# Retrieval spread over eight tiles a head instead of nine, with ScalarE's share written as a loop

## The reference

```
q = (ht @ w_q).reshape(T, 8, 2, 128)                  # 8 heads
s1, s2 = q[:, :, 0] . k1, q[:, :, 1] . k2              # 128 scores each
v1, i1 = top_k(s1, 16); v2, i2 = top_k(s2, 16)
cand = v1[..., :, None] + v2[..., None, :]             # 256 candidates
sc, flat = top_k(cand, 16)
idx = i1[flat // 16] * 128 + i2[flat % 16]
gate = softmax(sc)
act = gelu(x . u_tab[idx]); out = (gate * act) . v_tab[idx]
```

## Time and profile before

| what | value |
|---|---|
| median of three runs | 1848.8 us (1847.82 to 1850.55) |
| the profiled execution, its own time | 1851.15 us |
| its span | 1849.5 us |
| PE busy | 1812.2 us, 98% |
| DVE busy | 1423.3 us, 77% |
| ACT busy | 895.1 us, 48% |
| POOL busy | 513.9 us, 28% |

### The profile page before, as it was taken

The page is one execution under the profiler, slowest core; times in us unless marked ns, Lnnn a source line. Parts: engine busy times, 40 slices in busy tenths (PEclk is TensorE's granted clock), DMA queues, the critical chain, the costliest instruction groups (busy, mean ns, idle before and its releaser), DMA issues.

```text
span 1849.5 us, 37505 instructions
## 1 busy us (share of the span) xinstructions
PE 1812.2 (98%) x13425; PEld 1680.1 (91%) x13425; DVE 1423.3 (77%) x2638; ACT 895.1 (48%) x1337; POOL 513.9 (28%) x393
## 2 busy tenths in 40 slices
PE   6999999999999999999999999999999999999998
PEld 6999999999999888888889999999999988888887
DVE  7996688997666888788878767999766598875555
ACT  3345455554444444455544545555544444445553
POOL 1000036777760211000000001777777111110000
PEclk9999999999999999999999999999999999999999
DMA  8998777767664766788845744667766566665552
GB/s 315 335 333 313 254 255 218 187 175 192 174 161 162 246 225 225 270 335 317 317 146 170 265 165 163 189 175 184 189 170 170 165 231 224 224 234 193 193 193 91
DMA packets 145385, 404.26 MB, mean 219 GB/s; under 512 B 47008, under 2 KB 47392, under 8 KB 144672
## 3 DMA queue, kind: packets, MB, share of 16 engines
q1 hardware_dynamic: 105456, 384.21, 59.3%
q0 software_dynamic: 39424, 16.93, 7.7%
q10 hardware_dynamic: 432, 2.23, 0.3%
HBM read 383.25 MB, written 20.05 MB: 218 GB/s over the span
## 4 chain that ended last, share of the span: by engine, by line
PE 90%; DVE 7%; DMA 1%; issue 1%; ACT 1%; SPq 0%; DVEq 0%; ACTq 0%
PE ps L1295 47%; PE acc L1455 37%; PE gp L1410 2%; DVE acts L682 2%; DVE low L661 2%; PE gp L1209 1%; PE gp L1399 1%; PE ps L1269 1%; DVE acts L737 1%; DMA acts<-w_mod 1%; DMA raw<-conv_out 0%; DMA mov_h<-table 0%; PE gp L1231 0%; DVE mov_l L743 0%; ACT high L453 0%
## 5 line engine op out<-in xcount | busy, mean ns | idle before, releaser
L661 DVE TENSOR_TENSOR low<-raw,high 128x1024 fp32r<-128x1024 f32 x596 | 726.9, 1222 | 370.0 <-ACT high L453 359.5
L453 ACT ACTIVATE high<-raw 128x1024 fp32r<-128x1024 f32 x593 | 626.1, 1056 | 434.1 <-PE acc L1455 338.3
L1295 PE MATMUL ps<-mov_h,high 128*128 128x256 f32 x2640 | 752.5, 285 | 8.5 <-DVE acts L1065 2.5
L1295 PE MATMUL ps<-mov_h,low 128*128 128x256 f32 x2640 | 748.4, 283 | 0.0
L1295 PE MATMUL ps<-mov_l,high 128*128 128x256 f32 x2640 | 748.3, 283 | 0.0
L418 POOL DMA_INDIRECT table<-added x256 | 440.0, 1719 | 776.1 <-DVE added L878 633.7
L1295 PEld LDWEIGHTS ps<-mov_h,high 128*128 128x128 f32 x2640 | 507.8, 192 | 11.1 <-DVE low L661 4.4
L1295 PEld LDWEIGHTS ps<-mov_l,high 128*128 128x128 f32 x2640 | 508.0, 192 | 0.0
L1295 PEld LDWEIGHTS ps<-mov_h,low 128*128 128x128 f32 x2640 | 507.9, 192 | 0.0
L1455 PE MATMUL acc<-high,mov_h 128*128 128x512 f32 x1024 | 401.1, 392 | 1.0 <-DVE mov_l L1133 0.8
L1455 PE MATMUL acc<-high,mov_l 128*128 128x512 f32 x1024 | 398.7, 389 | 0.0
(11 more groups left out here) (129 smaller groups left out, 989.7 us busy)
## 6 DMA issues: line engine op xcount, KB each, us to landing
raw<-up SPq DMA_DIRECT2D x256, 512.0 KB
raw<-down SPq DMA_DIRECT2D x256, 512.0 KB
acts<-w_mod SPq DMA_DIRECT2D x84, 512.0 KB, 5.0
raw<-query SPq DMA_DIRECT2D x32, 512.0 KB
table<-hot SPq DMA_DIRECT2D x32, 512.0 KB, 6.5
raw<-conv_in SPq DMA_DIRECT2D x24, 512.0 KB
mov_h<-table POOLq DMA_DIRECT2D x96, 128.0 KB, 3.7
acts<-w_mod SPq DMA_DIRECT2D x6, 1024.0 KB, 15.1
```

The source lines that it names most:

```text
L453: nc.scalar.activation(flat(high[s]), tile_row(s), ACT.Copy).then_inc(high_ready, 1)
L661: nc.vector.tensor_tensor(flat(low[n % RING]), tile_row(n % RING), flat(high[n % RING]).bitcast(F32), ALU.subtract).then_inc(low_ready, 1)
L1295: ins = nc.tensor.matmul(dst, w[s][:, c], m[:, mv], start=(first and n == 0), stop=(last and n == 2), skip_group_check=skip)
```

## The change

DVE's `retrieval` loses the `beside()` at the end of each head, so a head spans eight tiles. The order of all other steps is kept. ACT's part for tiles 8 to 71 becomes a loop of eight trips of eight tiles, each with one exponential ahead of the rounding of its third tile, that is at tile 8p + 10. The wait for the re-loaded Gelu table moves behind the loop. Tiles 72 to 91 become a loop of four tiles (`gelus`), and 92 to 127 stay as they were. PE's, SP's and POOL's programs are the same, and so is `FIRST_SET`.

```
+            def ahead8(i, n0, s):
+
+                t = s + AHEAD
+                arrived(i * 2 + (n0 // RING + t // RING + 1), t % RING)
+                act.wait_ge(product, i * 8 + (n0 + t + 1))
+                nc.scalar.activation(flat(high[t % RING]), tile_row(t % RING), ACT.Copy).then_inc(high_ready, 1)
...
-                exps = {(HEADS + 1) * p + 11: p for p in range(HEADS)}
-                for j in range(8, TURN + 2 * HEADS):
-                    if j in exps:
-                        p = exps[j]
-                        act.wait_ge(soft_in, HEADS * layer + p + 1)
-                        sc = SC[:, TC * p * TOPK:TC * (p + 1) * TOPK]
-                        nc.scalar.activation(sc, sc, ACT.Exp).then_inc(soft_exp, 1)
-                        load_table(ACT.Gelu)
-                    gelu(0, j - j % RING, j % RING)
+                warm_count[0] += HEADS
+                with act.Fori(0, HEADS) as i:
+                    for j in range(8):
+                        if j == 2:
+                            act.wait_ge(soft_in, i + (HEADS * layer + 1))
+                            sc = A[:, bass.ds(i * (TC * TOPK) + o, TC * TOPK)]
+                            nc.scalar.activation(sc, sc, ACT.Exp).then_inc(soft_exp, 1)
+                            nc.scalar.activation(warm[:], eps[:], ACT.Gelu).then_inc(warmed, 1)
+                        ahead8(i, n0 + 8, j)
+                        act.wait_ge(product, i * 8 + (n0 + 8 + j + 1 + RING))
+                        nc.scalar.activation(A[:, bass.ds(i * (8 * T) + (8 + j) * T, T)],
+                                             ps[:, j % 2, 0:T], ACT.Gelu).then_inc(evac_act, 1)
+                act.wait_ge(warmed, warm_count[0])
+                gelus(8 + 8 * HEADS, (TURN + 2 * HEADS - 8 - 8 * HEADS) // RING)
...
                     for _ in before:
                         pass
-                    beside()
                     before = numbers(p)
```

## The result

The changed kernel took 1855.38 us (median of five, 1853.28 to 1858.52) against 1848.8 us: ratio 1.0029, 95% interval 1.0015 to 1.0043. The two medians are 6.6 us apart, and a ratio of 1.0029 is 5.4 us of 1848.8. I had forecast 1848.8 and no change. It is slower by a little more than the 0.2% that I had called measurable, and 1855.4 lies above my range.

The account below looks back on a forecast made before the run. PE, busy 98% of the span, was taken as the bound. All terms (DVE, ACT's wait, loop, POOL and SP, stops) summed to 0 us, so the median stayed at 1848.8 us, range 1843.1 to 1854.

Parts of the forecast that it names:

- DVE's pace: DVE's retrieval work of 22.71 to 22.88 us a head fits barely under PE's 23.04 for eight tiles; cost 0.
- Rival D: Eight tiles a head are too few for DVE, which becomes the bound: 1855.4 us, chance 0.05.
- ACT's wait for the scores: ACT's exponential waits for DVE's `soft_in`; moved a tile earlier, it keeps 1.80 us of its 4.68 to spare; cost 0.
- The loop: ACT's jump back costs 0.13 us, seven a layer cost ACT 0.9 us and PE nothing.
- The rival of a stalling jump: ACT's jump back stalls for an instruction fetch, hidden below 4 us; at 6 us, 1877 us in all; chance 0.05.
- The stops: Late ACT Gelus beside POOL's first transfers, layer 0: 5.74 us could return or be lost again; taken as unchanged, 0.
- a stop meets the next exponential: An ACT stop directly ahead of an exponential makes the next Gelu overrun its room by 0.75 us: 1849.6 to 1854.5, chance 0.08.
- Theory S: Formed for the experiments: the change costs nothing itself, acting only through ACT's stops beside POOL's first transfers; no chance given.

Follow-up runs that it names:

- e9: The changed kernel, unaltered, timed a third time against the kernel before, on chip 12: ratio 1.0000 (0.9991 to 1.0009).
- e11: The changed kernel, unaltered, timed a fourth time against the kernel before, on chip 1: ratio 1.0020 (1.0011 to 1.0029).
- e7: The changed kernel, unaltered, timed once more against the kernel before, on chip 2: ratio 0.9997 (0.9988 to 1.0006).
- e3: The changed kernel with head 0's transfers adding in place of writing, against the kernel before, on chip 3: ratio 0.9978 (0.9961 to 0.9996).
- e4: The kernel before with head 0's transfers adding in place of writing, against the kernel before, on chip 3: ratio 0.9975 (0.9958 to 0.9993).
- e13: Eight tiles a head with ACT written out, no loop, against the kernel before, on chip 14: ratio 1.0003.
- e14: Nine tiles a head with ACT's tiles 8 to 79 as two trips of 36, against the kernel before, on chip 14: ratio 1.0001.
- e16: Eight tiles a head with ACT written out, no loop, against the kernel before, on chip 7: ratio 1.0000.
- e17: Nine tiles a head with ACT's tiles 8 to 79 as two trips of 36, against the kernel before, on chip 7: ratio 1.0001.
- e1: Eight tiles a head with ACT written out, no loop, against the kernel before, on chip 3: ratio 1.0012 (0.9992 to 1.0032).
- e15: The kernel before with all heads' transfers writing, against the kernel before, on chip 14: ratio 1.0000.
- e18: The kernel before with all heads' transfers writing, against the kernel before, on chip 7: ratio 1.0001.
- e10: The changed kernel with its exponentials two tiles later, at 8p + 12, against the kernel before, on chip 12: ratio 1.0014 (1.0005 to 1.0023).
- e12: The changed kernel with all heads' transfers writing, against the kernel before, on chip 1: ratio 1.0415 (1.0372 to 1.0458).

## Why the prediction was wrong, point by point

**DVE's pace, 0 us: right.** DVE's timeline of e9, layer 1, to be held against the earlier trace rows:

```profile
1161.36 0.19 DVE L954 TENSOR_TENSOR acts<-acts 128x32 f32<-128x32 f32 x1
1161.82 1.22 DVE L673 TENSOR_TENSOR low<-raw,high 128x1024 fp32r<-128x1024 f32 x1
...
1167.48 1.23 DVE L673 TENSOR_TENSOR low<-raw,high 128x1024 fp32r<-128x1024 f32 x1 [0.27 <-ACT high L470]
...
1190.52 1.23 DVE L673 TENSOR_TENSOR low<-raw,high 128x1024 fp32r<-128x1024 f32 x1 [0.33 <-ACT high L470]
```

The idle time at the third `low` is 0.27 to 0.33 us (0.2 to 0.3 forecast), and its chain has the 72 tiles of layer 1 in one piece, `1111.09 207.35`, as before. A head's work is 22.71 to 22.77 us (23.04 less the idle time), at the lower end of my figure. Rival D is refuted: a kernel whose DVE has 1.4% to spare is as fast as one with 8% to spare, on every chip without stops.

**ACT's wait for the scores, 0 us: right.** ACT's timeline of e9:

```profile
1163.05 0.38 ACT L602 ACTIVATE acts<-ps 128x256 f32 x1 [1.54 <-PE ps L1306]
1163.45 1.28 ACT L598 ACT_TABLE_LOAD   x1
...
1166.40 1.05 ACT L470 ACTIVATE high<-raw 128x1024 fp32r<-128x1024 f32 x1
1167.35 0.36 ACT L602 ACTIVATE acts<-ps 128x256 f32 x1
...
1180.33 0.38 ACT L602 ACTIVATE acts<-ps 128x256 f32 x1 [1.55 <-PE ps L1306]
1180.75 1.06 ACT L470 ACTIVATE high<-raw 128x1024 fp32r<-128x1024 f32 x1
...
1186.49 1.28 ACT L598 ACT_TABLE_LOAD   x1
```

DVE's last step ends at 1161.55, the table load starts at 1163.45: 1.90 us to spare, 1.80 forecast. Exponentials are 23.04 us apart. The Gelu behind one is 1.42 us late (1165.93 would be on time), a little less than the 1.55 of before.

**The loop, 0 us where there are no stops: right.** At a trip's edge the rounding starts 0.42 us after the Gelu (1180.33 to 1180.75), 0.41 forecast. The table loads of e9, by line, stay two a head:

```profile
L598 ACT ACT_TABLE_LOAD x16 | 20.5, 1283 | 0.3
L599 ACT ACT_TABLE_LOAD x16 | 20.5, 1283 | 0.3
```

The rival of a stalling jump is refuted at eight tiles a trip. The Trainium skill (Runtime: NRT & Kernel Launch, Instruction fetch mechanics) describes a stall for a target outside the fetched window; no row here shows one, and none tells whether this loop's target lies outside it.

**The stops, "I take neither": the step that failed.** I had seen that the only movable time was in ACT's stops and had given both bounds. I set the term to 0 because the exponential of head 1 moved away from them and that of head 2 into them, and I counted it for layer 0 alone, since the stop of layer 1 had cost PE nothing. The runs showed a loss in its place: 5.4 us by the ratio in the first measurement, and 3.4 us in the mean (1854.56 against 1851.16) on chip 1. Layer 1, which I had put at nothing, lost 1.74 us in the profile after and 1.73 in e11, at the Gelus at 1153.88 and 1166.67 and at 1153.47 and 1166.29. Layer 0 lost 2.46 and 3.6 where 5.74 were before, so it moved towards the bound that gives time back.

The rival "a stop meets the next exponential" (0.08) had the layer and the size about right (0.75 us and up against 1.7), but not the mechanism. It has PE wait for the Gelu behind the exponential. In the profile after, PE's wait of 1.02 us ended with the stopped Gelu itself, ahead of the exponential, and from 1167.11 on PE ran in one piece, past the table load at 1168.29 and the late Gelu behind it (1172.18). That stopped Gelu was due at about 1163.3 (PE's piece starts at 1154.31, three tiles and the 0.4 us from a tile's end to its Gelu): 3.3 us late, which is over the ordinary room of 2.4 with no exponential in it. The kernel before shows the same in layer 0, where PE waited 1.95 us for the Gelu at 279.68, 11 us ahead of the next exponential. The sum over both layers is 4.2 us in the profile after against 5.74 before, so single executions don't give the +5.4. With a spread of 16 us on chip 3, they can't.

My reading was too sure in another way. I took the stops for a fixed property of the kernel, seen in one execution. Four of the six chips with a number show none in their profiles, and there the forecast, no change, holds within 0.1% in two series (e7, e9). Theory S stands in this form: the changed kernel was measured slower only in series whose profiles show stops. For it speak e3 against e4, e7, e9 and the parts alone in e13, e14, e16 and e17. Its other part, that a stop costs PE where it falls next to an exponential, is not shown.

**What stays open.** Why the changed kernel loses more to the stops than the kernel before is not settled. In layer 1 both kernels with nine tiles lost 0 and 0.5 us and all with eight tiles 1.7 to 4.1, loop or not. In layer 0 it is the other way: 5.74 and 9.8 us with nine tiles, 2.5 to 3.6 with eight. The exponentials' place alone doesn't explain it. In the kernel before, head 1's exponential stands 3.4 us behind POOL's first transfer in layer 0 (255.88 to 259.30) and 3.5 in layer 1 (1145.14 to 1148.69), and the one layer lost 5.74 us and the other nothing. Where stops occur, they keep their distance to POOL's first transfer rather than to the exponentials: some 12, 19 and 24 us in layer 0 of the kernel before (268.35, 274.50, 279.68) and in layer 1 of the profile after (1153.88, 1160.80, 1166.67, the first transfer at 1142.32). All of this is from single executions, and e1's timed interval reaches from 0.9992 to 1.0032. No series with stops had the kernel before with all heads writing (e15 and e18 met none), so whether nine tiles are less exposed is open too. Nor is it known what the first comparison compared: the runs of before (1846.3 to 1850.6) lie where before lies on chips without stops, those of after (1853.3 to 1858.5) where it lies on chip 1 (1851.7 to 1856.5). Some of the 0.29% may be chips and not kernels. Against this, the profile of before comes from an execution with stops, of 1851.15 us. Chip 1's 0.20% (0.11 to 0.29), from one chip for both, is the safer figure.

## What to carry to other kernels

An engine that paces a bound PE can be filled to 99% of its time (22.71 of 23.04 us here) if its latest step keeps its distance; follow one period step by step, and follow both sides of every hand-over (e10 lost on the side that I had not followed). When a profile shows idle time whose named releaser had long been done, treat it as a source of scatter, not as a constant: profile another execution and another chip before a small forecast leans on it. Here the better change is one word. With head 0's transfers adding, both kernels are 0.2% faster than the kernel before on chip 3, which has the stops; e4 and e3 are alike, so the change that was studied is neither needed nor harmful then.

## What the hardware showed that I had not expected

ACT's waits for PE's semaphore ended late, with up to 5.8 us of idle time where 1.6 is usual, while POOL issued indirect transfers of 128 four-byte elements in the writing form, in the first measurement and on chips 1 and 3. They did not in the adding form on chip 3 (e3, e4), nor in the writing form on chips 2, 7, 12 and 14. With sixteen heads writing the kernel took 4.15% more than the kernel before on chip 1 and 0.03% more on chip 2. PE's gap of 0.43 us inside a chunk (e12) shows that at least there no late semaphore was the reason. Whether ACT's stops are of the same kind can't be told from these traces, nor why the series differ.
